# Two transformer blocks on one core: layer 0 begun by halves of the features, norms tile by tile, conditioning rows on TensorE

## The reference

```
for layer in (0, 1):
    ada = silu(c) @ w_ada[layer] + b_ada[layer]           # 3072 values: shift, scale, gate
    h = rms_norm(x, g) * (1 + scale) + shift
    y = even_mixer(h) if layer == 0 else odd_mixer(h)     # projections, attention, silu gate, output projection
    x = x + gate * y
x = rms_norm(x, final_g)
u = rms_norm(x, mix_norm_g) @ w_in        # q, k, v, two convolution branches, three gates
x = x + merged(stick-breaking attention, 31-tap convolution, 3-tap convolution) @ w_o
gt, up = split(rms_norm(x, ffn_norm_g) @ w_ffn_in)
return x + (silu(gt) * up) @ w_ffn_out
```

## Time and profile before

| what | before |
|---|---|
| median of three timed runs | 909.75 us |
| the profiled execution | 912.89 us |
| its span, first to last instruction | 911.1 us |
| mean granted TensorE clock | 0.933 |
| TensorE busy | 799.6 us |
| VectorE busy | 539.4 us |
| ScalarE busy | 382.0 us |

### The profile page before, as it was taken

How to read it: one execution, slowest core, us unless ns; L and a number is a source line. 1 busy time by engine, 2 the same in 40 slices (tenths; PEclk the granted TensorE clock), 3 DMA queues, 4 the chain that set the end, 5 groups by cost and what they waited for, 6 DMA issues and landing times.

```text
span 911.1 us, 12018 instructions
## 1 busy us (share of the span) xinstructions
PE 799.6 (88%) x4898; PEld 675.7 (74%) x4898; DVE 539.4 (59%) x770; ACT 382.0 (42%) x582; POOL 25.4 (3%) x35
## 2 busy tenths in 40 slices
PE   3699789886979899777699999999989699999998
PEld 0378577334858777656597999988867699999886
DVE  3666478565376584754759879964642555445541
ACT  1342355334253544442534434458711544444330
POOL 2000001000000000000002000000000000000000
PEclk9889799986979899799699999999999799999999
DMA  9744554355045353330553555553221344444521
GB/s 356 278 163 161 218 199 140 139 191 225 1 146 223 139 185 139 139 139 0 208 185 139 192 188 180 181 186 138 93 93 47 138 183 182 178 186 180 203 93 46
DMA packets 20726, 145.77 MB, mean 160 GB/s; under 512 B 2352, under 2 KB 2512, under 8 KB 3648
## 3 DMA queue, kind: packets, MB, share of 16 engines
q1 hardware_dynamic: 19872, 142.32, 42.5%
q0 software_dynamic: 528, 1.65, 0.6%
q10 hardware_dynamic: 272, 1.05, 0.3%
HBM read 143.95 MB, written 1.05 MB: 159 GB/s over the span
## 4 chain that ended last, share of the span: by engine, by line
PE 48%; DVE 5%; ACT 1%; issue 1%; POOL 0%; DVEq 0%; ACTq 0%
PE banks L406 14%; PE banks L407 14%; PE banks L408 14%; PE banks L455 5%; DVE WL L1336 1%; DVE QT L1709 1%; ACT WH L948 1%; DVE HL L1402 1%; PE banks L786 1%; PE banks L811 1%; DVE ROT L1394 0%; PE banks L797 0%; ACT HH L977 0%; DVE MS L1720 0%; DVE QR L1729 0%
## 5 line engine op out<-in xcount | busy, mean ns | idle before, releaser
L1336 DVE TENSOR_TENSOR WL<-RAW,WH 128x2048 fp32r<-128x2048 f32 (+1 forms) x101 | 228.5, 2279 | 52.2 <-ACT WH L948 51.8
L948 ACT ACTIVATE WH<-RAW 128x2048 fp32r<-128x2048 f32 (+1 forms) x101 | 192.1, 1907 | 151.3 <-PE banks L408 97.0
L406 PE MATMUL banks<-HH,WH 128*128 128x256 f32 x832 | 239.5, 288 | 10.3 <-DVE HL L1402 6.5
L407 PE MATMUL banks<-HL,WH 128*128 128x256 f32 x832 | 238.7, 287 | 0.0
L408 PE MATMUL banks<-HH,WL 128*128 128x256 f32 x832 | 238.4, 287 | 0.0
L406 PEld LDWEIGHTS banks<-HH,WH 128*128 128x128 f32 x832 | 163.4, 196 | 11.3 <-DVE HL L1402 7.3
L407 PEld LDWEIGHTS banks<-HL,WH 128*128 128x128 f32 x832 | 163.3, 196 | 0.0
L408 PEld LDWEIGHTS banks<-HH,WL 128*128 128x128 f32 x832 | 163.1, 196 | 0.0
L406 PE MATMUL banks<-WH,HH 128*128 128x512 f32 (+1 forms) x304 | 123.7, 407 | 19.7 <-DVE HL L1532 8.1
L407 PE MATMUL banks<-WL,HH 128*128 128x512 f32 (+1 forms) x304 | 121.1, 398 | 0.0
L408 PE MATMUL banks<-WH,HL 128*128 128x512 f32 (+1 forms) x304 | 120.8, 397 | 0.0
(11 more groups left out here) (233 smaller groups left out, 882.7 us busy)
## 6 DMA issues: line engine op xcount, KB each, us to landing
RAW<-in_weights_dram SPq DMA_DIRECT2D x130, 1024.0 KB, 4.8
RAW<-in_weights_dram SPq DMA_DIRECT2D x2, 816.0 KB, 4.4
X<-in_x_dram ACTq DMA_DIRECT2D x1, 1024.0 KB, 5.7
QT<-in_weights_dram SPq DMA_DIRECT2D x1, 1024.0 KB, 11.7
V<-in_weights_dram SPq DMA_DIRECT2D x1, 1024.0 KB, 16.9
ZS<-in_weights_dram SPq DMA_DIRECT2D x1, 1024.0 KB, 20.8
out_dram<-X SPq DMA_DIRECT2D x2, 512.0 KB, 2.7
BIG<-in_final_g_dram POOLq DMA_DIRECT2D x1, 512.0 KB, 12.1
```

The costliest lines, as they stand in the source:

```text
L406: pe.matmul(out_, lhsT=w[0], rhs=x[0], start=start, stop=False, **more)
L407: pe.matmul(out_, lhsT=w[0], rhs=x[1], start=False, stop=False, **more)
L948: do(act.activation(WH[:, s % SPLIT_RING, 0:kb * width], RAW[:, slot[n] % RAW_RING, 0:kb * width], ACT.Copy), high_done)
L1336: do(dve.tensor_tensor(WL[:, s % SPLIT_RING, w], RAW[:, slot[n] % RAW_RING, w], WH[:, s % SPLIT_RING, w], ALU.subtract), low_done)
```

## The change

**Rows.** `ada` on VectorE is gone. All twelve conditioning rows go through TensorE: the matmul of block k writes partitions 32k to 32k+31 (the column of CACT broadcast to 32 columns), `row_in` adds all 128 partitions to ACC, and `conditioning` and `gate_rows` sum with QUADS, which is 1 in the rows 0, 32, 64 and 96 and 0 elsewhere. Rows (0,4) and (0,5) stand in steps 2 and 3 of layer 0's attention, (1,0) to (1,3) in steps 7 to 10, (1,4) and (1,5) in steps 0 and 4 of layer 1's attention. Layer 1's columns are made inside output(0), after its first tile.

**Start.** Rows 0 and 2 give shift and scale of the first 512 features; these features of both tiles are evicted (`first_evict(0)`), and the first halves of kcks and kakw (pieces kcks.0, kakw.0) are multiplied, with the row halves (0,1), (0,3) between them; then the second halves. The identity alone is loaded first; the other constants, the sinks and final_g come later on GpSimd's queue.

**Norms.** In n1, n2 and n3, tile 0 is turned inside the projection (`norm_turn` before the fourth tile y.1.1), evicted and used for two token tiles, while tile 1 is added, normed and turned. For this, q2 and k2 come before val and cga, and the first two blocks of the feed-forward part are computed by tokens (`hidden_tokens`), gated, and turned back (`hidden_turn`). VectorE's weight parts for the first two token tiles stand between its own norm steps. The 31 taps begin with v2. Q and k of layer 1 and of the second block are taken tile by tile.

The diff's core:

```diff
@@ piece_table @@
-    t = between(0, 0, 1) + between(0, 2, 3) + rows("kcks") + two("kakw", KB // 2, 408, "rows")
+    first = list(zip(rows("kcks"), two("kakw", KB // 2, 408, "rows")))
+    t = ada(0, 0, 2) + list(first[0]) + ada(0, 1, 3) + list(first[1])
...
-    t += cols("za", "zb") + ada(0, 4, 5) + ada(1, 1, 0, 3, 2) + rows("wo0_0", "wo0_1")
+    t += cols("za", "zb") + ada(0, 4, 5) + ada(1, 0, 1, 2, 3) + rows("wo0_0", "wo0_1")
...
-    t += cols("val", "cga") + rows("q2", "k2", "v2") + cols("scx", "scg", "sbg", *(f"g{i}" for i in range(6)))
+    t += rows("q2", "k2") + cols("val", "cga") + rows("v2") + cols("scx", "scg", "sbg", *(f"g{i}" for i in range(6)))
@@ TensorE @@
+            def conditioning_half(layer, c, half, kind="proj"):
+                use, name = f"cols{layer}.{c}", f"ada{layer}_{c}"
+                bank = tiles[ps.uses[use][0]] if half else ps.open(pe, kind, use)
+                wait_raw(pe, name, half)
+                w = raw(name, half)
+                for k in range(KB // 2):
+                    kk = half * KB // 2 + k
+                    mm = pe.matmul(bank[32 * k:32 * k + 32, :], lhsT=CACT[:, kk:kk + 1].to_broadcast([P, 32]),
+                                   rhs=w[:, k, :], start=(half == 0), stop=(half == 1))
+                if half:
+                    ps.fill(mm, use)
+                    readers[index[(name, half)]] = ps.filled_at(use)
+                else:
+                    mark_read(mm, name, half)
...
+            def conditioning(layer, use, chunks, kind="proj"):
+                bank = ps.open(pe, kind, use)
+                for c in chunks:
                     ps.wait_drained(pe, f"cols{layer}.{c}")
-                bank = ps.open(pe, "proj", f"ada{layer}")
-                for j in range(2 * KB):
-                    mm = pe.matmul(bank[:, j:j + 1], lhsT=ACC[:, j * P:(j + 1) * P], rhs=ONES[:, 0:1],
-                                   start=True, stop=True)
-                ps.fill(mm, f"ada{layer}")
+                    for j in range(4 * c, 4 * c + 4):
+                        mm = pe.matmul(bank[:, j:j + 1], lhsT=ACC[:, j * P:(j + 1) * P], rhs=QUADS[:, 0:1],
+                                       start=True, stop=True)
+                ps.fill(mm, use)
...
                         by_tokens(f"wo{layer}_{c}" if layer < 2 else f"wf{c}", t, use=f"y{layer}.{t}.{c}")
+                        if (layer, t, c) == (0, 0, 0):
+                            conditioning(1, "ada1", (0, 1, 2, 3))
+                        if (t, c) == (1, 0):
+                            norm_turn(layer + 1, 0)
...
+            def half_tokens(name, half, t, width, kind="proj"):
+                use = f"{name}.{t}"
+                bank = tiles[ps.uses[use][0]] if half else ps.open(pe, kind, use)
+                pe.wait_ge(ht_low, 2 * half + t + 1)
+                wait_parts(pe, name, half)
+                wh, wl = parts(name, half)
+                for k in range(KB // 2):
+                    kk = half * KB // 2 + k
+                    mm = product(bank[:, 0:width], [h[:, kk, t * P:(t + 1) * P] for h in (HH, HL)],
+                                 [wh[:, k, 0:width], wl[:, k, 0:width]], kk == 0, kk == KB - 1)
+                if half == 0 and t == NT - 1:
+                    mark_read(mm, name, 0)
+                if half == 1:
+                    ps.fill(mm, use)
+                    if t == NT - 1:
+                        readers[index[(name, 1)]] = ps.filled_at(use)
+            conditioning_row(0, 0, "out")
+            pe.wait_ge(ident_in, 16)
+            norm_turn(0, 0)
+            norm_turn(0, 1)
+            conditioning_row(0, 2, "out")
+            pe.wait_ge(quads_set, 4)
+            conditioning(0, "ada0.0", (0, 2), "out")
+            half_tokens("kcks", 0, 0, 512)
+            conditioning_half(0, 1, 0, "out")
+            half_tokens("kcks", 0, 1, 512)
+            conditioning_half(0, 1, 1)
+            half_tokens("kakw", 0, 0, 408, "turn")
+            conditioning_row(0, 3, "out")
+            conditioning(0, "ada0.1", (1, 3), "out")
+            half_tokens("kakw", 0, 1, 408, "out")
+            half_tokens("kcks", 1, 0, 512)
+            half_tokens("kcks", 1, 1, 512)
+            pair_turn(0)
+            half_tokens("kakw", 1, 0, 408)
+            pair_turn(1)
+            half_tokens("kakw", 1, 1, 408)
...
-                          7: [lambda: conditioning_row(1, 1)], 8: [lambda: conditioning_row(1, 3)]})
+                          7: [lambda: conditioning_row(1, 0)], 8: [lambda: conditioning_row(1, 1)],
+                          9: [lambda: conditioning_row(1, 2)], 10: [lambda: conditioning_row(1, 3)]})
             pe.wait_ge(ot_low, KB)
             output(0)
-            norm(1, 2)
+            normed(1, 0)
+            by_tokens("q1_0", 0)
+            norm_turn(1, 1)
+            by_tokens("k1_0", 0)
             normed(1)
...
-            attention(1, {0: [lambda: by_features("z1_0", 0), lambda: by_features("z1_0", 1)],
+            attention(1, {0: [lambda: by_features("z1_0", 0), lambda: conditioning_row(1, 4),
+                              lambda: by_features("z1_0", 1)],
...
-                          4: [lambda: by_features("z1_1", 0)], 6: [lambda: by_features("z1_1", 1)]})
+                          4: [lambda: by_features("z1_1", 0), lambda: conditioning_row(1, 5)],
+                          6: [lambda: by_features("z1_1", 1)]})
...
+            normed(2, 0)
+            by_tokens("q2", 0)
+            norm_turn(2, 1)
+            by_tokens("k2", 0)
             normed(2)
...
+            by_tokens("k2", 1)
+            qk_turn(1)
+            by_features("val", 0)
+            qk_turn(2)
+            by_features("val", 1)
+            qk_turn(3)
...
+            normed(3, 0)
+            hidden_tokens(0, 0)
+            norm_turn(3, 1)
+            hidden_tokens(1, 0)
             normed(3)
-            for i in range(FB // 2):
+            hidden_tokens(0, 1)
+            hidden_tokens(1, 1)
+            for i in range(2, FB // 2):
                 by_features(f"fi{i}", 0, use=f"fg.{i}")
+                if i == 2:
+                    hidden_turn(0)
+                    hidden_turn(1)
                 by_features(f"fi{i}", 1, use=f"fu.{i}")
@@ ScalarE, the start and norm 1 (norms 2 and 3 in the same order) @@
+            highs(1)
+            first_evict(0)
+            highs(2)
+            first_evict(1)
+            highs(4)
...
+            act.wait_ge(x_new, 2)
+            square("n1", 0)
+            act.wait_ge(mod_ready, 3)
+            evict_norm(1, 0)
+            highs(first_split("q1_0") + 2)
+            act.wait_ge(x_new, 4)
+            square("n1", 1)
+            highs(first_split("k1_0") + 2)
+            evict_norm(1, 1)
@@ VectorE @@
-            def ada(name, half):
-
-                layer, c = int(name[3]), int(name[5])
-                w = raw(name, half)
-                wait_raw(dve, name, half)
-                dve.wait_ge(bias_in, 16 * (layer + 1))
-                acc = ACC[:, c * 512:(c + 1) * 512]
-                for k in range(KB // 2):
-                    kk = half * KB // 2 + k
-                    do.after()
-                    do(dve.scalar_tensor_tensor(acc, w[:, k, :], CACT[:, kk:kk + 1], acc, ALU.mult, ALU.add),
-                       ada_read if k == KB // 2 - 1 else None)
...
-                acc = ACC[0:1, c * 512:(c + 1) * 512]
-                ps.drain(dve.tensor_tensor(acc, acc, bank[0:1, :], ALU.add), use)
+                acc = ACC[:, c * 512:(c + 1) * 512]
+                ps.drain(dve.tensor_tensor(acc, acc, bank[:, :], ALU.add), use)
...
+            def output_and_norm(layer, first_name, second_name):
+                add_output(layer, 0, 0)
+                if layer == 0:
+                    modulation(1, "ada1", slice(0, KB))
+                add_output(layer, 0, 1)
+                hat_after(layer, 0)
+                add_output(layer, 1, 0)
+                evict_norm(layer + 1, 0)
+                lows(first_split(first_name) + 2)
+                add_output(layer, 1, 1)
+                hat_after(layer, 1)
+                lows(first_split(second_name) + 2)
+                evict_norm(layer + 1, 1)
...
+            row_in(0, 0)
+            row_in(0, 2)
+            modulation(0, "ada0.0", slice(0, KB // 2))
+            first_evict(0)
+            lows(1)
+            low_norm(0, 1, 0, ROT2, 2)
+            lows(2)
+            row_in(0, 1)
+            row_in(0, 3)
+            modulation(0, "ada0.1", slice(KB // 2, KB))
+            first_evict(1)
+            low_norm(0, 1, 1, ROT2, 4)
+            lows(4)
```

604 lines of the change are left out of this document (319 added, 285 removed).

## The result

The changed kernel takes 900.89 us (median of 6 runs, 897.77 to 905.21), the kernel before 909.55 in the same hours: a ratio of 0.9907, interval 0.9887 to 0.9927. The direction was forecast, the size was not: 8.7 us came where 23.5 were forecast, and the time lies 1.9 us above the range. Two later executions stand far off, at 2650 us in row04_low and 4250 us in six_orders; the medians given here leave them out (with them they are 898.59 and 867.07).

A forecast was written before the change was run, and what follows sets the result against it. TensorE, busy 799.6 of 911.1 us, was taken as the bound. Gains of 7.5 + 11.9 + 3.5 - 11.9 + 3.5 + 1.5 + 7.5 = 23.5 took 912.9 to 889.4, on the median's terms 886 (range 875 to 899).

The forecast's parts named there:

- the bank at z1_0: Layer 1's attention: row (1,4) makes z1_0.1 wait for a projection bank that ScalarE frees late; -10.9 us.
- Start: Kernel start by halves: products from 26.1 us instead of 47.73, then an idle of 5.3; gain 7.5 us (3 to 11).
- Layer 0 attention: Layer 0's attention: steps 7 to 10 become four steps of 5.0 us; gain 11.9 us (6 to 15).
- The tail: End of layer 0's attention: a chain of highs, lows and a 5 us piece; 20.2 us from step 11, before 19.1.
- Norm 1: Norm after output(0), done by tile: two token tiles run while tile 1 is normed; gain 3.5 us (1 to 6).
- Layer 1 attention: Layer 1's attention: -10.9 us for the bank, -1.0 for row (1,5); together -11.9 (-14 to -3).
- Norms 2 and 3, q2 and k2: Later norms by tile, gains 3.5 and 7.5 us; q2 and k2 lose their waits for QR, gain 1.5.
- (b): Rival: the norms by tile bring nothing, two low parts delay the second tile; 14.5 us lost, 900; chance 0.14.
- (c): Rival: short idles keep TensorE at 1.2 GHz a tile more, at start and three norms; 10 lost, 896; chance 0.13.
- (a): Rival: the bank at z1_0 costs little, as ScalarE gets its piece earlier; 877 us; chance 0.10.
- (d): Rival: the start by halves gives nothing, as the second halves' highs come last; 7.5 lost, 893; chance 0.05.
- (e): Rival: the rows' quarters on TensorE don't overlap, a row takes 6.9 us; 933 us in all; chance 0.03.

The follow-up runs named there:

- row04_low: Changed kernel with row (0,4) in a bank of the kind out and zb.1's low part made in step 1 instead of step 2: 897.97 us.
- six_orders: Changed kernel with row14_bank, key_first, tail_heads, row04_low, gate_first and start_high together: 862.02 us, ratio 0.9534 to the kernel before.
- start_high: Changed kernel with the highs and lows of kcks.1 and kakw.1 ahead of the second halves' modulation at the start: 895.03 us.
- row04_bank: Changed kernel with row (0,4) opening a bank of the kind out instead of kc2's projection bank: 899.42 us.
- norm1_whole: Changed kernel with norm 1 undone: output(0) in one go, q, k, v tiles in the old order: 899.23 us.
- key_first: Changed kernel with ScalarE evicting v1_0.1 and the last key turn before it makes the next high: 897.47 us.
- row14_bank: Changed kernel with row (1,4) opening a bank of the kind out instead of a projection bank: 891.84 us.
- rows_only_bank: Kernel before with only the eight rows (0,4) to (1,5) in quarters on TensorE, row (1,4) in a bank of the kind out: 904.20 us against 908.39.
- gate_first: Changed kernel with z1_1.0's eviction, tanh and probability copies ahead of the high of wo1_0.1's piece, which moves to step 5: 893.53 us.
- tail_heads: Changed kernel with the highs and lows of wo0_1's pieces behind the last heads of layer 0's attention: 892.93 us.

## Why the prediction was off

Four steps failed, and no single one carries the miss: norm 1's gain was let run past the key turn's wait, the rows in steps 2 and 3 of layer 0 were priced at full clock, the start behind its first products was priced too low, and row (1,5) was charged for a delay but not for itself. The costliest step of the forecast, the bank at z1_0, was right.

**Start (7.5 forecast, 5.0 found; ten profiles: 4.3 to 6.7).** Products begin at 25.6 (26.1; the terms that I listed add up to 25.5), and the idle comes where and as long as I said (5.0; 5.3). It ends 0.7 us late, since a half row takes 1.04 us and more where I had 0.85. Another 0.6 is lost up to qa's second tile at 71.4: kcks.1's products alone take 8.37 us behind the idle, and 5.75 in start_high. The last 1.3 lie behind that, 0.8 of it in the records after the wait for w1v.1, which were granted 0.58 in this trace and 0.88 before. start_high shows what the idle costs: 3.5 us of it gone gave 5.7.

**Layer 0 attention (11.9; 8.7).** Steps 7 to 10 went as written, with rows of 1.9 to 2.3 us. The tail was right to the tenth (20.2 from step 11). The failed term is steps 2 to 6: I had 3.8 us lost, 6.1 were. Row (0,4)'s wait for kc2's bank is there (2.25), but both rows then run at half clock, 3.4 and 3.6 us for 1.9. The wait of 3 us for row (0,5)'s pieces was not there. The late row (0,4) hid it: row04_bank brought out 1.7 us of it, and row04_low removed them. The trace also had luck: steps 7 to 11 took 20.95 of a mean of 22.6.

**Norm 1 (3.5; 0.4).** The mechanism was right up to the third tile: at O+49.0 with two tiles done, forecast O+48. The failed step is the one that I did not write: from there I let the gain run on. But the q, k, v tiles end with a key turn whose eviction stands on ScalarE behind a high, and that high waits for its piece until 282.1, 75.3 us after output(0) (before 75.8). The chain of pieces had hardly become shorter. TensorE arrived earlier and waited 5.6 us instead of 3.3. The changed kernel, then the kernel before:

```profile
282.09 1.91 ACT L1012 ACTIVATE WH<-RAW 128x2048 fp32r<-128x2048 f32 x1 [5.74 <-DMA RAW<-in_weights_dram]
```

```profile
296.18 1.91 ACT L948 ACTIVATE WH<-RAW 128x2048 fp32r<-128x2048 f32 x1 [5.33 <-DMA RAW<-in_weights_dram]
...
299.37 1.65 PE L548 MATMUL banks<-KT,QT 64*128 64x128 f32 x8 [3.31 <-ACT KT L986]
```

norm1_whole and key_first show both halves of this.

**Layer 1 attention (-11.9; -13.7).** The step that costs was found and nearly sized: idle 6.96 (forecast 6 to 8), half clock to 308, the second scores 11.0 us later than the shift said (10.9, though the terms as written add up to 10.7). Over eleven profiles the stretch costs 9.8. row14_bank and rows_only_bank confirm the term in two kernels. Row (1,5) cost 2.6 and not 1.0, and the mechanism was wrong. I had charged its first half's delay of the release; but the wait in step 4 is shorter than before, 5.1 us for 6.0. What costs is the row's own 1.9 us on the path, and step 4's products, 7.1 us for 5.9, which begin at half clock in this trace.

**Norms 2 and 3, q2 and k2 (12.5; 11.6).** The idles at the three norms' turns and first tiles sum to 16.3 us; before they were 30.8. Norm 3 gave 8.2 (7.5). The stretch with norm 2, q2 and k2 gave 3.4 (5.0), but these terms were right: from output(1) to the turn of V in the second block's attention it took 201.3 us instead of 206.3, a gain of 4.9. The other 1.6 were lost behind that turn, in code that the change does not touch, on records that ran partly at half clock (granted 0.69 over 608.3 to 613.8). The changed kernel, then the kernel before:

```profile
608.37 5.41 PE L453 MATMUL banks<-KT,RAW 128*128 128x256 f32 x16
```

```profile
613.67 3.72 PE L455 MATMUL banks<-KT,RAW 128*128 128x256 f32 x16
```

That is chance: of the seventeen kept profiles six have the long form and eleven the short one, each after the same idle of 1.3 us, and gate_first, with the same code there, has the short one. Norms 2 and 3 were not tested alone.

**The offset (0; 3.3).** The gains were read from an execution 3.3 above its median and taken off the median whole.

Of 14.8 us missed, 3.3 are the offset, 3.2 layer 0's attention, 3.1 norm 1, 2.5 the start, 1.8 layer 1, and 0.9 the rest (1.6 lost by chance, 0.7 won by norm 3). None alone puts the time outside the range, and with any one of the first four put right it would have lain inside. That the time is the 900 of rival (b) is luck: (b) took all three norms to bring nothing, and it is near the truth for norm 1 alone. A share of (c) holds, for the start and for rows (0,4) and (0,5), which are also the two rows over 3 us that I had named as a sign. Rivals (a) and (d) are false (the start gave 5.0), and (e) is priced nearly rightly and false.

## What to carry to other kernels

A gain is worth what is left of it at the next in-order wait: follow it to the first eviction that stands behind a transfer, and end it there. When a step is inserted, ask which bank or slot it takes in turn and who frees that; here one bank out of turn cost 9 us, more than the rows gained. An engine that both prepares weights and evicts results should not stand for a transfer ahead of an eviction that TensorE waits for: key_first and gate_first each put such an eviction first, and tail_heads the last heads' parts. It is no rule that evictions come first, as start_high gained by the opposite order. Six edits of order and bank, none of which changes any arithmetic, gave four times what the change gave, and three of the waits that they mend stand in the kernel before as well (3.3, 6.0 and 6.6 us).

## What the runs showed of the hardware

Records of 512 columns in four column quarters run four at once: 1.92 us for sixteen, 7.03 one partition at a time. Their starts show it: four within 0.02 us, the next four 0.43 later.

The page "TensorEngine Tiling (Array Packing)" of the Trainium skill, Key Properties, says that a change of tiling mode drains TensorE. The trace agrees, with about 0.09 us a change. In the row at 166.98 the groups start 0.43 apart, but the next records, of another shape, start 0.52 after the last group. Turns (128*128) start 0.11 us apart, while from the last turn to the first scores (64*128) it is 0.20, in sixteen places of the changed kernel. One change shows none, from the masks to a row. My prediction said that no such cost shows, because the ends of the records overlap the next starts; those ends are modelled, and the starts are what to read. It is small beside a row.

The clock falls after short idles that I had not charged: 0.55 granted over row (0,4), behind an idle of 2.25 us in which nothing ran, and then 3.36 us for a row instead of 1.92. It need not: after 1.54 us in start_high it was 1.00, and after 1.3 us in the second block's attention the next products ran partly at half clock in six profiles of seventeen. Nor does it take an idle. Row (0,5) ran at 0.53 over 137.4 to 141.0, behind the compressed scores, 32 records of 15 columns. row04_low tells them from an idle: TensorE does not idle between its step 1 and this row, row (0,4) takes 1.92 us at 1.00, the granted clock is 0.88 over the compressed scores (128.8 to 132.5) and 0.50 over row (0,5) behind them. So there the clock fell in the small records, with no idle.

Idle time that went away returned 1.1 to 1.7 times its length where it returned any (key_first 4.6 us of idle for 4.9 of stretch, tail_heads 4.8 for 5.9, gate_first 5.1 for 6.2, start_high 3.5 for 5.7 and row14_bank 5.1 for 8.6, the last two against the mean of the other profiles). In row04_bank 2.25 us returned nothing.
